# Three panels behind the first norm and at the first feed-forward, and transposed blocks copied ahead of the row maximum

## The reference, cut to what matters

```
layer l = 0, 1:  proj = x @ w_in, cut into the inputs of four branches
   a: banded attention, 4 heads, own chunk + 8 chunks back, bias table
   c: banded attention, rope, 2 chunks back, sinks
   b: latent attention: q = rms_norm(c_q) @ w_uq, kv = rms_norm(c_kv) @ w_ukv,
      rope on 32 columns, softmax over all keys up to the query's chunk
   m: attention on a memory of 256 rows
   x = layer_norm(alpha * x + concat(branch * silu(gate)) @ w_out)
second block:    x = x + 0.5 * swiglu(rmsnorm(x), w_ffn1_gu, w_ffn1_down)
                 mixer (recurrence + neighbourhood attention) and its w_out
                 x = x + 0.5 * swiglu(rmsnorm(x), w_ffn2_gu, w_ffn2_down)
```

## Time and profile before

| | |
|---|---|
| median of 3 runs | 3425.94 us |
| profiled execution, its own time | 3428.1 us |
| its span | 3426.3 us |
| TensorE matmuls busy | 3338.8 us, 97% |
| VectorE, ScalarE, POOL busy | 1564.8, 961.9, 1531.4 us |
| DMA | 194.28 MB |

### The profile page before, as it was taken

The page is one execution under the profiler, slowest core; times in us unless marked ns, Lnnn a source line. Parts: engine busy times, 40 slices in busy tenths (PEclk is TensorE's granted clock), DMA queues, the critical chain, the costliest instruction groups (busy, mean ns, idle before and its releaser), DMA issues.

```text
span 3426.3 us, 48542 instructions
## 1 busy us (share of the span) xinstructions
PE 3338.8 (97%) x19500; PEld 1699.8 (50%) x19500; DVE 1564.8 (46%) x2397; ACT 961.9 (28%) x1776; POOL 1531.4 (45%) x988
## 2 busy tenths in 40 slices
PE   8999998999999899999999999999999999999999
PEld 4555653655654344444445554555554444444444
DVE  4365458145547733333113376666566653333100
ACT  1433422234332400000002455555554310000000
POOL 4556652446664233333333566555565433333332
PEclk9999999999999999999999999999999999999999
DMA  3122112112121111111222011111112111111112
GB/s 130 40 52 61 58 61 96 44 44 70 35 76 39 37 49 50 54 49 48 70 69 93 29 58 51 50 51 52 52 35 92 54 38 54 49 49 55 45 51 83
DMA packets 55197, 194.28 MB, mean 57 GB/s; under 512 B 7408, under 2 KB 7792, under 8 KB 54512
## 3 DMA queue, kind: packets, MB, share of 16 engines
q1 hardware_dynamic: 52576, 182.96, 17.2%
q10 hardware_dynamic: 2448, 8.91, 0.7%
HBM read 172.97 MB, written 12.58 MB: 54 GB/s over the span
## 4 chain that ended last, share of the span: by engine, by line
PE 93%; DVE 3%; issue 2%; ACT 1%; POOL 1%; DMA 0%; DVEq 0%; POOLq 0%; ACTq 0%
PE pair L1078 27%; PE pair L1079 26%; PE pair L1080 26%; PE pair L1298 3%; PE pair L1267 2%; PE pair L1279 2%; PE pair L1467 1%; PE pair L1493 1%; PE pair L1478 1%; PE pair L1421 1%; PE pair L1098 1%; PE pair L1256 0%; DVE arena L1985 0%; DVE arena L1938 0%; DVE residual L1938 0%
## 5 line engine op out<-in xcount | busy, mean ns | idle before, releaser
L1078 PE MATMUL pair<-operand,panel_parts 128*128 128x512 f16 x2752 | 1048.6, 381 | 40.2 <-DVE operand L1938 26.3
L1079 PE MATMUL pair<-operand,panel_parts 128*128 128x512 bf16 x2752 | 1046.3, 380 | 0.0
L1080 PE MATMUL pair<-operand,panel_parts 128*128 128x512 f16 x2752 | 1046.0, 380 | 0.0
L883 POOL TENSOR_SCALAR panel_parts<-panel_raw 128x1024 f16<-128x1024 f32 (+3 forms) x280 | 284.7, 1017 | 1430.8 <-PE pair L1080 973.3
L884 POOL TENSOR_TENSOR panel_parts<-panel_raw,panel_parts 128x1024 bf16<-128x1024 f32 (+3 forms) x280 | 646.5, 2309 | 23.4
L1078 PE MATMUL pair<-arena,panel_parts 128*128 128x512 f16 (+2 forms) x1200 | 453.5, 378 | 8.4 <-issue 4.6
L1078 PEld LDWEIGHTS pair<-operand,panel_parts 128*128 128x128 f16 x2752 | 269.6, 98 | 386.2 <-issue 96.6
L920 POOL TENSOR_SCALAR arena<-arena,row_inv 128x256 f32<-128x256 f32 (+7 forms) x256 | 344.4, 1357 | 246.7 <-DVE row_inv L2004 246.7
L1079 PE MATMUL pair<-arena,panel_parts 128*128 128x512 bf16 (+2 forms) x1200 | 452.2, 377 | 0.0
L1080 PE MATMUL pair<-arena,panel_parts 128*128 128x512 f16 (+2 forms) x1200 | 452.1, 377 | 0.0
L1080 PEld LDWEIGHTS pair<-operand,panel_parts 128*128 128x128 bf16 x2752 | 270.0, 98 | 327.1 <-issue 3.9
(11 more groups left out here) (219 smaller groups left out, 3964.0 us busy)
## 6 DMA issues: line engine op xcount, KB each, us to landing
panel_raw<-in_wgu SPq DMA_DIRECT2D x88, 512.0 KB, 3.5
panel_raw<-in_wl SPq DMA_DIRECT2D x58, 512.0 KB, 3.6
panel_raw<-in_wm SPq DMA_DIRECT2D x56, 512.0 KB, 3.6
panel_raw<-in_wdn SPq DMA_DIRECT2D x32, 512.0 KB, 3.6
residual<-residual_spill SPq DMA_DIRECT2D x15, 512.0 KB, 6.9
panel_raw<-in_wl SPq DMA_DIRECT2D x18, 384.0 KB, 3.2
panel_raw<-in_wdn SPq DMA_DIRECT2D x16, 384.0 KB, 3.1
residual<-in_xT ACTq DMA_DIRECT2D x8, 512.0 KB, 11.5
```

The lines of the kernel that those rows point to most:

```text
L883: chained(nc.gpsimd.tensor_scalar(hi[:, c], RAW[:, s, c], HI_MAX, -HI_MAX, ALU.min, ALU.max))
L1078: nc.tensor.matmul(out, stat[0], mov[0], start=first, stop=False)
L1079: nc.tensor.matmul(out, stat[0], mov[1], start=False, stop=False)
L1080: return nc.tensor.matmul(out, stat[1], mov[0], start=False, stop=last)
```

## The change

It has three parts.

1. The second query panel of branch a, `aq1`, leaves the filler list of branch a (T falls from 198 to 182 steps) and joins `first_panels` with weights and PSUM of its own (`HOME["aq1"]`, `SECOND_QUERY`, the two transposing banks). In the second layer it is interleaved per k tile with the other two, in the first layer done behind them. ScalarE copies it out at the first piece of `ag0`; the first `slot_turn` of the layer waits for that.
2. In `ffn(1)` panels 0, 1 and 2 are interleaved per k tile.
3. In branch b, where the next slot is also one of b, VectorE copies group 1's transposed blocks before the row maximum of the next slot's group 1.

```diff
-    "a": ["aq1", "ak1", "av1", "ag1", "bq0", "bq1", "bkv", "cq0", "ss_q", "ss_kv", "cq1", "ck", "cv", "cg0"],
+    "a": ["ak1", "av1", "ag1", "bq0", "bq1", "bkv", "cq0", "ss_q", "ss_kv", "cq1", "ck", "cv", "cg0"],
...
-                panels += [("aq0", l), ("ak0", l)]
-                panel_at["ak0", l] = l, -1, 0
-                last_piece["ak0", l] = None
+                panels += [("aq0", l), ("ak0", l), ("aq1", l)]
+                for name in ("ak0", "aq1"):
+                    panel_at[name, l] = l, -1, 0
+                    last_piece[name, l] = None
...
-        HOME = {"av0": parts(12288, 1024), "mq0": parts(5120, 1024)}
+        HOME = {"aq1": parts(14336, 1024), "av0": parts(12288, 1024), "mq0": parts(5120, 1024)}
...
+        SECOND_QUERY = PS[:, 1536:2560]
...
+                    layer_panel(l, "aq1")
...
-                elif n >= 2 and name != "av0":
+                elif n >= 2 and name not in HOME:
...
+                    elif last == "aq1":
+                        used = second_query_ready, k + 1
...
+                def second_query(w, k):
+                    for c in range(2):
+                        m = product(SECOND_QUERY[:, cols[c]], pick(w, ALL, slice(k * P, (k + 1) * P)),
+                                    pick(xp, ALL, slice(k * T + cols[c].start, k * T + cols[c].stop)), k == 0, k == KT - 1)
+                    return m
...
-                m.then_inc(first_key_ready, 1)
+                    if k == KT - 1:
+                        m.then_inc(first_key_ready, 1)
+                    if l > 0:
+                        if k == 0:
+                            w2 = layer_weights("aq1", l)
+                        m = second_query(w2, k)
+                if l == 0:
+                    w2 = layer_weights("aq1", l)
+                    for k in range(KT):
+                        m = second_query(w2, k)
+                m.then_inc(second_query_ready, 1)
...
+                if s.n == 0 and g == 0:
+                    pe.wait_ge(second_query_kept, l + 1)
...
-                dsts = [acquire(f"gu{idx}", 0, j) for j in range(2)]
+                together = 3 if idx == 1 else 2
+                dsts = [acquire(f"gu{idx}", 0, j) for j in range(together)]
...
-                    for j in range(2):
+                    if together == 3 and k == 0:
+                        weights(f"gu{idx}", 0, 2)
+                        ws.append(THIRD_FFN[idx])
+                    for j in range(together):
...
-                gu(0, 2, THIRD_FFN[idx])
+                if together == 2:
+                    gu(0, 2, THIRD_FFN[idx])
...
+                    if name == "ag0" and c == 0:
+                        act.wait_ge(second_query_ready, l + 1)
+                        copy(AQ[1], SECOND_QUERY, HD ** -0.5).then_inc(second_query_kept, 1)
...
-                    if nxt == "b":
+                    if nxt == "b" and s.branch != "b":
                         slot_row_max(n + 1, 1)
                     slot_keep(n, 1)
+                    if nxt == "b" and s.branch == "b":
+                        slot_row_max(n + 1, 1)
```

More of the change, by code:

```diff
@@ L521, in build @@
         first_key_kept = sem("first_key_kept")
+        second_query_ready = sem("second_query_ready")
+        second_query_kept = sem("second_query_kept")
         first_half_split = sem("first_half_split")
@@ L1234, in slot_scores_of @@
                     if s.branch == "a":
-                        layer_piece_kept(pe, f"aq{s.pair}", l)
                         if s.pair == 0:
+                            layer_piece_kept(pe, "aq0", l)
                             pe.wait_ge(first_key_kept, l + 1)
```

## The result

The changed kernel takes 3438.67 us, median of 6 runs (3435.67 to 3439.12), beside 3425.02 for the kernel before, median of 6 run beside it. The ratio is 1.0038, with a 95% interval of 1.0028 to 1.0047: 10 to 16 us slower. The forecast was 3432 with a range of 3420 to 3437, so the sign of its sum was right, the size too small, and the measured time lies 1.7 us beyond the range. The profiled executions differ by 10.7 us (spans 3426.3 and 3437.0), where the prediction's sum was 6.4.

What follows compares the result with a forecast made beforehand. TensorE, 93% of the chain that ended last, was taken as the bound. The terms summed to +6.4 on the profiled 3428.1 us, so 3434.5; less 2.2 to the median, 3432.3, called 3432, range 3420 to 3437.

Steps and rivals of the forecast that it cites:

- Part 2, -2.0: First feed-forward: three interleaved panels close TensorE's waits for tiles from k = 5 on; -2.0 us, bounds -2.1 and 0.
- Part 3, -4.1: Branch b: the copy ahead of the row maximum starts earlier, saving 2.1 us a layer, -4.1 in both; bounds -6.5 and 0.
- The roots, +7.3: Slot 11, branch a: the shorter filler list puts the roots ahead of ScalarE's copy; TensorE stalls 3.65 us a layer, +7.3.
- The clock behind the stall, +4.2: Behind the stall in slot 11 the granted clock falls and matmuls slow: 2.1 us a layer, +4.2; bounds 0 and 5.8.
- Smaller shifts, +1.0: Slots 8 to 14: squares and VectorE's chain of 13 move earlier, ahead of copies; +1.0 us, bounds 0 and 2.
- under `av0` and `ag0`: Behind the first norm: new SP order, POOL order and ScalarE's 1 us copy are covered by 20.7 us of matmuls.
- Part 1's own gain, -0.4: Behind the first norm, second layer: one wait of 0.19 us (0.36 real) goes; -0.4 us, nothing in the first layer.
- The 0.4 for the fewer steps in the first fill: First fill has 2 steps, not 3, so transposes wait for POOL's first scaling: 0.2 us a layer, +0.4.
- Rival A: The roots cost nothing, through slack or enough TensorE work; 7.3 and 4.2 leave the sum, 3421 us; chance 0.17.
- rival C: Branch b: the later row maximum is paid back, so the 4.1 us gain goes; 3436.5 us, chance 0.12.
- Rival B: The stall in slot 11 comes but the clock holds; sum +2.2, 3428 us, chance 0.16.

Runs made afterwards that it cites:

- part 1 alone: The changed kernel with parts 2 and 3 undone, so only part 1 on the kernel before: 3442.83 us, ratio 1.0049 to the kernel before.
- e6: The kernel before with only the two roots placed two parts early, in part 0 of slot 11: 3436.77 us, ratio 1.0027 to the kernel before.
- e7: The changed kernel with second-layer POOL split of `aq1` behind the first x tile and TensorE's `aq1` two k tiles later: 3445.15 us, ratio 1.0055 to before.
- e1: The changed kernel with the roots and the chain of normalise two parts later, in their old parts: 3427.99 us, ratio 1.0009 to the kernel before.
- e5: The changed kernel with the roots and the chain of normalise one part later: 3430.84 us, ratio 1.0010 to the kernel before.
- e2: The kernel before with only branch b's copy of group 1 put ahead of the next row maximum: 3421.00 us, ratio 0.9986 to the kernel before.

## Why the prediction came out too low, step by step

**Part 2, -2.0: right.** -1.7 to -2.4 in the stages. The split of panel 3 did move behind the additions, as the prediction had it: the six additions took 7.53 us, not the 10.04 of the earlier trace rows, and the split began 1.5 us after they had ended.

```profile
1177.55 7.53 DVE L1972 TENSOR_TENSOR stats<-stats,arena 128x1024 f32<-128x1024 f32 x6
...
1186.58 1.04 POOL L889 TENSOR_SCALAR panel_parts<-panel_raw 128x1024 f16<-128x1024 f32 x1 [41.07 <-PE pair L1088]
...
1190.80 0.39 PE L1086 MATMUL pair<-operand,panel_parts 128*128 128x512 f16 x1 [1.39 <-DVE arena L1996]
```

**Part 3, -4.1: right,** and to 0.1: 2.13 + 1.99.

**The roots, +7.3: right.** Read between starts the stalls are 3.60 and 3.59, 7.2 in all, against 3.65 each. By the page that the prediction set beside it (the Trainium skill, ScalarE: Activation LUTs, What ACT_TABLE_LOAD costs) 1.38 us of drain would come on top; the root starts 0.01 behind the load's end, and the stall is no longer than the sum without it, so at this load the traces do not show it.

**The clock behind the stall, +4.2: too much of one kind.** The prediction said that the clock fell behind every idleness over 2 us. It did not: behind the same 3.43 it was 0.75 in one profile of the changed kernel and 1.00 in the other (above), and behind the 2.02 of the norm 0.72 before and 1.00 after. The norm's two stretches, before and then after:

```profile
529.87:535.87 6.00, 6.00 (x16) 2.34 (x17) 5.26 (x4) 0.00 (x0) 1.83 (x1) 0.72 0.54 190
```

```profile
538.06:544.06 6.00, 6.00 (x24) 2.70 (x25) 5.90 (x5) 0.00 (x0) 1.83 (x1) 1.00 0.31 87
```

Over five profiles with the stall (two of after, part 1 alone, e6, e7) the clock fell behind 7 of 10. Where it fell, 5 to 8 matmuls ran 0.43 apart and the transposes between them slowed too. From the stall's end to the next scores it was 5.57 us in the second profile of after and in e7, where the clock held, and 7.05 to 7.26 where it fell (8.24 once, in part 1 alone): 1.5 to 1.7 a fall, once 2.7. Seven falls in ten stalls make some 2.4 for both layers, an estimate, not 4.2; in the first profile of after both stalls were followed by a fall, 3.2 in all.

The 1.9 us extra in the first panels is the same chance: behind 2.44 of idleness at 16.13 the clock was 0.75, where the kernel before had idled only 1.21 and kept 1.00. Four kernels without part 1 took 58.46 to 61.26 there, beside 57.49 for before. In part 1 alone that stretch, from the first matmul behind the wait (17.25) to the first scores, is 51.83, against 41.36 with part 3 alone: the 10.34 of the moved steps and 0.1.

**Smaller shifts, +1.0: the step that failed.** This term took VectorE's operations at their undisturbed duration and moved them by place alone. But the pieces moved, POOL's splits follow the pieces, and the VectorE operations that began beside a split ended only behind it, two to three times as long as alone. The kernel before already showed this behind the very wait of 0.33 in the earlier trace rows: the operation ahead of that copy took 2.70 us, where its kind takes 1.22 at 201.31.

```profile
194.97 2.70 DVE L1941 SCALAR_TENSOR_TENSOR residual<-residual 128x1024 f32<-128x1024 f32 x1
...
193.61 2.98 POOL L884 TENSOR_TENSOR panel_parts<-panel_raw,panel_parts 128x1024 bf16<-128x1024 f32 x1
```

In the changed kernel two places in the slots show it, and a third stands behind the norm (below). Slot 4 of the first layer, VectorE and then POOL and TensorE:

```profile
114.38 2.06 DVE L2259 TENSOR_SCALAR arena<-arena 128x1024 f32<-128x1024 f32 x1
116.48 0.29 DVE L2048 COPY stats<-pair 128x128 f32<-128x128 f32 x1
...
113.76 2.13 POOL L890 TENSOR_TENSOR panel_parts<-panel_raw,panel_parts 128x1024 bf16<-128x1024 f32 x1
...
116.82 0.33 PE L1305 MATMUL pair<-ident,arena 128*128 128x128 f32 x1 [1.45 <-DVE stats L2048]
```

The rope step, 0.69 us alone in the kernel before (at 102.26), ends 0.55 behind the end of POOL's operation (115.89), so it can have done little until then, and the copy behind it makes TensorE wait 1.45. In slot 13 of both layers:

```profile
218.09 2.82 DVE L1975 SCALAR_TENSOR_TENSOR residual<-residual,layer_cols 128x1024 f32<-128x1024 f32 x1
220.83 0.28 DVE L2048 COPY stats<-pair 128x128 f32<-128x128 f32 x1
...
216.84 2.98 POOL L890 TENSOR_TENSOR panel_parts<-panel_raw,panel_parts 128x1024 bf16<-128x1024 f32 x1
...
221.37 0.44 PE L1324 MATMUL pair<-stats,arena 128*64 128x128 f32 x4 [0.94 <-DVE stats L2048]
```

1.23 us became 2.82, ending 1.1 behind the split's end at 219.82. The wait of 0.47 in slot 14 is of the kind that the prediction had priced: its copy stands behind two undisturbed operations of 1.21. Read between starts, the waits of slots 13 and 14 are 0.94 and 0.63, less the 0.50 of the earlier trace rows, so 1.1 a layer, and that of slot 4 is 1.5. Together they make 3.6. A remainder of 0.4 to 0.5 a layer, spread over a and c, I have not placed; it is there in e1 as well (0.4 in each layer), which has no stall and no fall of the clock in these stages. So the term measured 3.6 + 0.9 = 4.5, where the prediction had 1.0.

**A term that was missing: the norm, +1.8.** This is the second step that failed. The prediction put POOL's new work "under `av0` and `ag0`". The split of `aq1` for the second layer isn't there; it stands right behind that of `ak0`, ahead of the norm's last steps, and pushes the split of `av0` behind it. Before, `av0` was done at 565.0, ahead of these steps (VectorE at 567.23); now `aq1` takes 568.23 to 571.47, and the split of `av0` meets them. The first matmul of the second layer waits on them. VectorE, then POOL (`aq1`, then `av0`):

```profile
573.73 4.28 DVE L1975 SCALAR_TENSOR_TENSOR arena<-arena 128x1024 f32<-128x1024 f32 x2
578.05 2.36 DVE L1972 TENSOR_TENSOR residual<-residual,arena 128x1024 f32<-128x1024 f32 x2
...
569.35 2.12 POOL L890 TENSOR_TENSOR arena<-panel_raw,arena 128x1024 bf16<-128x1024 f32 x1
572.57 3.10 POOL L890 TENSOR_TENSOR arena<-panel_raw,arena 128x1024 bf16<-128x1024 f32 x1
583.55 0.59 PE L1086 MATMUL pair<-operand,panel_parts 128*128 128x512 f16 x1 [12.78 <-DVE operand L1972]
```

The pair took 2.48 before. In the five kernels of these runs without `aq1` there the idleness was 10.97 or 10.98; in the six profiles with it 12.77 or 12.78; in e7, which moved only the splits of `aq1` and `av0` behind the first tile, 10.97. One pair of profiles hides this, because the clock mixes in: without `aq1` the stretch with the first norm took 134.8 and 135.4 where the clock held behind the 2.02, and 136.5 to 137.4 where it fell; with `aq1` there it took 136.6 to 137.9 where the clock held and 139.5 where it fell.

The Trainium skill, SBUF — State Buffer, Who interferes with whom, says that a VectorE operation with two SBUF inputs contends with a GpSimd operation that reads SBUF, as does one in a mode that uses two ports, and that whichever starts first holds the shared ports for its whole instruction while the other waits. By that rule, the traces agree: VectorE ended 0.55, 1.1 and 2.3 us (two operations of 1.23) behind POOL's end in the three places, its own undisturbed time or less, and POOL's 3.10 instead of 2.13 begins under a VectorE operation that ends at 573.70. Whether the rope step, which has one input, is in a two-port mode no run here shows; that it is held does fit. Weighed ahead of the result, together with the order of POOL's splits before the second layer, the rule would have pointed at this missing term.

**Part 1's own gain, -0.4: nothing.** Against 56.16 (45.82 and the moved steps) the stretch took 56.1 to 57.0 in six profiles, on average 0.3 more. It follows the granted clock over its first six us: 56.06 at 0.69, 56.66 at 0.59, 56.97 at 0.53. Without part 1 it was 45.82 to 45.84 in four profiles with the clock at 0.71 to 0.77 (46.79 at 0.50). So the wait of the earlier trace rows may well be gone, but two panels left TensorE time between the tiles in which a low clock was caught up, and three do not. That last reason is argued from these rows, not tested. The 0.4 for the fewer steps in the first fill has no row of its own.

Put together, as expected over many executions: -2.0 - 4.1 + 7.2 + 2.4 (the clock, an estimate) + 3.6 + 0.9 (the remainder) + 1.8 + 0.3 (first panels of layer 2) = 10.1, where the prediction had 6.4; the two comparisons give 10 to 16 and 7 to 14. The two profiled executions differ by 10.7: there the falls behind both stalls made 0.8 more, the first panels came out 1.9 and 0.5 higher, the first norm 1.4 and the rest 1.2 lower, by the clock for the most part. Rival A fell with e5 and e6, rival C with e2. Rival B was half right: the clock held behind some of the stalls.

## What to carry to other kernels

Where side work is placed by the positions of a list, a shorter list moves all of it; follow each engine's moved operation to what stands behind it there, as was done for ScalarE, and do the same for POOL, since its splits move too and take VectorE's time where they meet. A gain should be weighed against what it displaces: part 1 aimed at 0.4 us of waits and cost some 17 (12 to 22 by its own run), while the two parts that moved nothing else gave what the rows of before said, and are the version to keep. When a change's time is near the scatter, distances between fixed rows of TensorE measure each part to 0.2 us, as long as the granted clock did not fall between them in one of the two profiles; look at it first.

## What was not expected of the hardware

The granted clock behind the same idle time is not the same from one execution to the next: 0.75 or 1.00 behind 3.43 us, 0.72 or 1.00 behind 2.02. Nor is a longer wait the surer one: behind the 1.57 us before the first scores it fell in four of the twelve profiles (0.72), behind the 1.65 at the end of branch c in none. A fall cost 1.5 to 1.7 us behind the stalls, once 2.7; how much of the scatter between executions it makes was not tested.

A VectorE operation beside a POOL split is held even when it is tiny: four columns of row maxima, 0.16 us in the changed kernel, took 1.38 in e1 and ended at 234.85, 0.01 behind such a split (233.19 to 234.84).

```profile
233.47 1.38 DVE L1972 TENSOR_TENSOR neg_max<-neg_max,negsink 128x4 f32<-128x4 f32 x1
```
